# Two attention units of tiles 2 and 3 share a lot for their scores in a one-core hybrid decoder step

## The chip, the cores and the metric

One core of a Trainium2 chip. The metric is the device time of one execution in microseconds (us), the median of several runs. The change is one table of numbers that places pieces of work in the kernel's written-out order; no instruction's shape changes.

## What is computed

The kernel does one inference step of a two-layer decoder on 512 prompt tokens (4 tiles of 128) and 8 sample tokens (a fifth, small tile). Layer 0 has differential attention, layer 1 a short gated convolution. Each is followed by a layer norm, an expert layer that looks 128 experts up for every token (8 heads, 16 experts each), another norm, and a gated embedding. What the change touches is the attention of the prompt tiles:

```
s = einsum('bqhcd,bkhcd->bchqk', q, k) * HD**-0.5 - slope * dist     # two score maps, c = 0, 1
p = softmax(s);  w = p[:, 0] - lam * p[:, 1]
o = einsum('bhqk,bkhv->bqhv', w, v)
```

and what it shares the engines with is the expert layer, whose rows `u_tab[idx]` and `v_tab[idx]` are gathered from HBM for every token:

```
a = einsum('td,thkd->thk', xt, u_tab[idx]);  hk = g * gelu(a)
out = einsum('thk,thkd->td', hk, v_tab[idx])
```

## The kernel before, in words

**Lots.** The expert layer sets the beat. One gather (`L989`, on GpSimd's queue) brings one expert row of u and v for each of a tile's 128 tokens, 128 x 2048 floats or 1 MB, into a ring of slots. Two gathers make a *lot*: VectorE takes the two dot products (`two_dots`, L1672, two of 128x1024), ScalarE the gelu, the gate and the scaling of the two v rows (`two_experts`, L1166 gelu, L1169, L1180), TensorE adds them into `acc` by 16 transposing products of 128x128 (`add_two`, L1919), which frees the two slots. A tile has 64 lots, so the lots of tiles 0 and 1 of layer 0 are counted 0 to 127 here. Up to gather 216 (lot 108) the ring has 8 slots, four lots: the gathers of lot t + 4 wait for the adds of lot t.

**Background.** All else (projections, attention, norms, routing for the next tile) stands in lots as *pieces*, in an order that `Plan.build` writes. TensorE does the pieces of lot t **before** its adds of lot t. ScalarE and VectorE do them **two lots behind** (`BEHIND = 2`): the pieces of lot t come after the expert work of lot t + 1 and before that of lot t + 2. Each engine works strictly in its order. A piece that ends in a PSUM bank takes the next of four banks in turn, so a product waits until the product four before it has been read (`bank_freed`); the reader is ScalarE or VectorE, in its own background.

**An attention unit** u is one head of one tile of 128 queries; units 16 to 23 are tile 2 and units 24 to 31 tile 3. It has four pieces:
- `score`: two products on TensorE (L1760), one bank each; VectorE adds the position bias and takes the maximum (L1334, L1342 twice, L1347), ScalarE two exponentials (L1070). Exp and gelu are in different function tables of ScalarE, so an `ACT_TABLE_LOAD` stands ahead of the exponentials and another ahead of the next gelu.
- `weigh`: VectorE combines the two maps (L1355, L1357, L1359).
- `w_turn`: TensorE transposes the weights, 3 or 4 blocks, into `tp` (L1771); ScalarE copies them (L1079). From unit 16 on all units use the same `tp` bank, so a unit's transposes wait for the copy of the unit before.
- `pv`: 3 or 4 products with the values (L1780), read by ScalarE (L1083, L1085).

From unit 16 on the score maps of units u and u - 2 share a buffer: VectorE's score step of u waits until TensorE has transposed u - 2 (`a_wT_ps`). Before the change the unit j of tile 2 has its scores in lot 36 + 7(j // 2) + 3(j % 2), that of tile 3 in lot 64 + 2j; `weigh` follows one lot later, `w_turn` four and `pv` seven. In the same lots lie the projections of tiles 2 and 3 (`qk` L1718, `v` L1752, `k_rows` L1731; up to lot 56), the routing of tile 1 (`route`, VectorE from L1502 to L1571), at lot 64 the change of tile (`back` L1981 and L1132, the copy of `acc` L1228), and at lots 72 and 90 the turning back of the heads (`o_back` L1787, L1092). The functions are `Plan.build`, and inside `build`: `logits`, `weights`, `lead`, `open_product`, `two_experts`, `add_two`.

Of the kernel before, what the change touches and what calls it, by code (L numbers as in the profile page):

```python
# [114 lines left out]
class Plan:  # L115
# [255 lines left out]
    def build(self):  # L371
# [71 lines left out]
        window(0, 1, (0, 10, r1[25:]), (14, 30, bg), (24, 32, r2[:13]))  # L443
        lots = steps[1][3] + steps[2][3]
        for j in range(HEADS):
            for b, at in ((2, 36 + 7 * (j // 2) + 3 * (j % 2)), (3, 64 + 2 * j)):
                u = b * HEADS + j
                lots[at] += self.score[u]
                lots[at + 1].append(self.weigh[u])
                lots[at + 4].append(self.w_turn[u])  # L450
                lots[at + 7].append(self.pv[u])
        for b, at in ((2, 68), (3, 86)):
            lots[at].append(self.o_root[b])
            lots[at + 1].append(self.o_scale[b])
# [1665 lines left out]
```

## Time and profile before

| | |
|---|---|
| median of 3 runs | 3188.34 us (3184.56 to 3188.4) |
| the profiled execution's own time | 3192.09 us |
| its span, first to last instruction | 3190.1 us |
| granted TensorE clock, mean | 0.874 |
| busy: TensorE, VectorE, ScalarE, GpSimd | 77%, 71%, 62%, 38% |
| DMA: mean rate, share of the gather queue | 394 GB/s, 84.9% |
| chain that ended last: DMA, TensorE, VectorE, ScalarE | 37%, 25%, 17%, 11% |
| `ACT_TABLE_LOAD` ahead of gelu, whole run | 111 of 1283 ns |
| ScalarE in a lot: gelu; two gates; two scalings | 203 ns; 286 ns each; 1141 ns each |
| VectorE in a lot: two dot products | 1222 ns each |

A time in the profile is counted from the span's start. Lot 36 begins (its first dot product) at 465.9, lot 64 at 639.7, lot 84 at 751.3. PE is TensorE, DVE VectorE, ACT ScalarE, POOL GpSimd. "[x <-y]" behind a row is how long the engine stood idle before it and what ended that.

### The profile page before, as it was taken

To read this page: it belongs to the slowest core of one execution; us is meant where nothing else is said; L and a number is where in the kernel's file an instruction comes from. 1 tells how busy PE (TensorE), PEld (TensorE's weight loads), DVE (VectorE), ACT (ScalarE), POOL (GpSimd) and SP (SyncE) were. 2 spreads that over 40 slices of the span, in tenths; PEclk is the share of its full clock that TensorE was granted. 3 is DMA by queue.
4 is the path that set the end of the run, shared out by engine and by line. 5 is a ranking of instruction groups with operands and counts; after the bars stand their busy time and mean duration, and the time that the engine had idled before them with its cause. 6 is when DMAs were issued, how large, how long until landed. Compare 5 with 4: busy or idle time off the path is not lost.

```text
span 3190.1 us, 42742 instructions
## 1 busy us (share of the span) xinstructions
PE 2449.7 (77%) x13752; PEld 2024.4 (63%) x13752; DVE 2259.8 (71%) x5825; ACT 1989.4 (62%) x3694; POOL 1221.5 (38%) x1095
## 2 busy tenths in 40 slices
PE   8886878766978777886877687888787565587777
PEld 6555767655777666775765566776576555546665
DVE  2625678886467877778856877677668888678655
ACT  1325567797566865556655796555656666657883
POOL 1113333434444443343434344334444444444341
PEclk9878989887989889898888898998799877877899
DMA  7558999989999999999999999999999999999996
GB/s 291 185 215 354 397 418 406 401 364 405 411 419 420 421 420 421 421 420 416 383 420 421 382 421 421 421 420 421 418 419 420 405 422 420 414 375 421 421 421 278
DMA packets 182544, 1256.05 MB, mean 394 GB/s; under 512 B 21359, under 2 KB 26223, under 8 KB 33585
## 3 DMA queue, kind: packets, MB, share of 16 engines
q0 software_dynamic: 156320, 1113.83, 84.9%
q1 hardware_dynamic: 24416, 136.35, 10.7%
q10 hardware_dynamic: 1584, 3.15, 0.3%
q8 instruction: 110, 1.80, 0.2%
q14 instruction: 114, 0.93, 0.1%
HBM read 1246.78 MB, written 6.50 MB: 393 GB/s over the span
## 4 chain that ended last, share of the span: by engine, by line
DMA 37%; PE 25%; DVE 17%; ACT 11%; issue 4%; DVEq 3%; ACTq 2%; POOL 1%; SPq 0%; POOLq 0%
DMA arena<-in_uv,idx 35%; DVE arena L1672 9%; PE acc L1919 8%; PE bank L1946 6%; ACT arena L1180 5%; PE bank L1937 4%; PE bank L1718 2%; PE bank L1752 1%; DMA panel<-in_panels 1%; POOL arena L989 1%; DVEq L1578 1%; ACT act_w L1169 1%; ACT L1166 1%; ACTq L1167 1%; ACT L1159 1%
## 5 line engine op out<-in xcount | busy, mean ns | idle before, releaser
L989 POOL DMA_INDIRECT arena<-in_uv,idx x1024 | 1176.1, 1149 | 1724.2 <-PE acc L1919 1496.9
L1919 PE MATMUL acc<-cst,arena 128*128 128x128 f32 x8128 | 1245.7, 315 | 631.5 <-ACT arena L1180 630.8
L1919 PEld LDWEIGHTS acc<-cst,arena 128*128 128x128 f32 x8128 | 1094.2, 163 | 804.2 <-ACT arena L1180 777.4
L1672 DVE CUSTOM_DVE_ANT_0 arena<-arena,h 128x1024 f32<-128x1024 f32 x1024 | 1230.3, 1222 | 491.5 <-DMA arena<-in_uv,idx 484.0
L1180 ACT ACTIVATE arena<-arena,act_w 128x1024 f32<-128x1024 f32 x1016 | 1112.0, 1141 | 37.0 <-issue 2.4
L1166 ACT ACTIVATE act_w<-dots 128x2 f32<-128x2 f32 x520 | 105.3, 203 | 840.0 <-DVE dots L1672 839.0
L1946 PE MATMUL bank<-hT,panel 128*128 128x264 f32 (+2 forms) x1856 | 431.5, 389 | 6.5 <-issue 6.5
L1946 PEld LDWEIGHTS bank<-hT,panel 128*128 128x128 f32 x1856 | 352.4, 201 | 58.4 <-issue 8.9
L1169 ACT ACTIVATE act_w<-act_w 128x1 f32<-128x1 f32 x1040 | 249.5, 286 | 44.3 <-issue 2.2
L1166 ACT ACT_TABLE_LOAD x111 | 142.4, 1283 | 1.6
L1718 PE MATMUL bank<-hT,panel 128*128 128x264 f32 (+1 forms) x512 | 120.7, 397 | 19.1 <-DMA panel<-in_panels 13.6
L1718 PEld LDWEIGHTS bank<-hT,panel 128*128 128x128 f32 x512 | 100.5, 199 | 35.9 <-DMA panel<-in_panels 14.4
L1937 PE MATMUL bank<-panel,qT 128*128 128x256 f32 (+1 forms) x448 | 108.7, 399 | 0.0
L1937 PE MATMUL bank<-panel,hT 128*128 128x256 f32 (+1 forms) x448 | 102.9, 384 | 0.7 <-ACT hT L1126 0.7
L1937 PEld LDWEIGHTS bank<-panel,qT 128*128 128x128 f32 (+1 forms) x448 | 82.1, 189 | 19.3 <-issue 3.3
L1937 PEld LDWEIGHTS bank<-panel,hT 128*128 128x128 f32 (+1 forms) x448 | 70.5, 162 | 25.1 <-issue 4.8
L1672 DVE DVE_READ_ACCUMULATOR2_ANT dots<- 128x1 f32 x1040 | 85.2, 82 | 0.0
L1502 DVE COPY yb<-tp 128x256 f32<-128x256 f32 x80 | 33.8, 422 | 65.1 <-PE tp L1861 60.8
L1937 PE MATMUL bank<-panel,arena 128*128 128x256 f32 x256 | 62.4, 403 | 7.5 <-DMA panel<-in_panels 6.7
L1070 ACT ACTIVATE h<-h,small 128x128 f32<-128x128 f32 (+3 forms) x64 | 35.4, 554 | 50.7 <-DVE small L1347 50.4
L1551 DVE TENSOR_TENSOR yb<-ya,cst 128x512 f32<-128x512 f32 x80 | 55.4, 692 | 11.4
L1937 PEld LDWEIGHTS bank<-panel,arena 128*128 128x128 f32 x256 | 51.3, 204 | 16.6 <-DMA panel<-in_panels 7.5
(241 smaller groups left out, 2262.2 us busy)
## 6 DMA issues: line engine op xcount, KB each, us to landing
panel<-in_panels SPq DMA_DIRECT2D x116, 1024.0 KB, 9.3
arena<-in_uv,idx POOLq DMA_INDIRECT x1024, 19.9
arena<-in_cache_k POOLq DMA_DIRECT2D x16, 512.0 KB, 6.6
arena<-in_cache_v POOLq DMA_DIRECT2D x16, 512.0 KB, 4.8
arena<-out_y_s POOLq DMA_DIRECT2D x8, 512.0 KB, 9.0
arena<-in_panels SPq DMA_DIRECT2D x4, 1024.0 KB, 8.2
h<-in_h SPq DMA_DIRECT2D x2, 1024.0 KB
out_y_p<-h SPq DMA_DIRECT2D x3, 512.0 KB
```

Of the source, the lines that this page charges most:

```text
L989: nc.gpsimd.indirect_dma_start(uv[:, slot_of(e), :], None, uv_dram[layer], bass.IndirectOffsetOnAxis(ids[:, r:r + 1], 0)).then_inc(gathere ...
L1070: e = nc.scalar.activation(logit(u)[:, c, 0:n], logit(u)[:, c, 0:n], ACT.Exp, bias=nb[:, u % 2, c:c + 1], scale=SCALE, accum_out=lsum[:, u ...
L1166: nc.scalar.activation(act_w[:, 1, half, s], dots[:, half, s], ACT.Gelu).then_inc(gelu_done, 1)
L1169: nc.scalar.activation(act_w[:, 2, half, r:r + 1], act_w[:, 1, half, r:r + 1], ACT.Copy, scale=act_w[:, 0, half, r:r + 1])
L1180: nc.scalar.activation(row, row, ACT.Copy, scale=act_w[:, 2, half, r:r + 1]).then_inc(weighted, 1)
L1502: V.tensor_copy(r_sc, tp[0][:, 0:256]).then_inc(sc_read, 1)
L1551: V.tensor_tensor(r_eq.rearrange("p (k i) -> p k i", i=16), r_ijf.rearrange("p (k i) -> p k i", i=1).broadcast_to([P, 32, 16]), const("iot ...
L1672: V.tensor_tensor_reduce(uv[:, slot_of(e), 0:D], uv[:, slot_of(e), 0:D], x_rows, 1.0, 0.0, ALU.mult, ALU.add, dots[:, G % 2, r:r + 1]).the ...
L1718: t = mm(product_of[:, 0:width], w[:, c, :], hT[:, c, 0:width], start=(c == 0), stop=(c == C - 1))
L1919: m = mm(acc[:, c * P:(c + 1) * P], uv[:, slot_of(e), D + c * P:D + (c + 1) * P], const("ident"), is_transpose=True, start=False, stop=Tru ...
L1937: last = mm(bank[0:m, x.n % BANKS, 0:PW], src[:, c, first:first + m], weights[:, c, :], start=(c == 0), stop=(c == chunks - 1))
L1946: last = mm(bank[:, x.n % BANKS, 0:width], w[:, c, :], hT[:, c, lo:lo + width], start=(c == 0), stop=(c == C - 1))
```

## The change

The scores of units 2i and 2i + 1 of a tile are placed in the same lot: in tile 2 in lots 36, 43, 50, 57 (the second unit three lots earlier than before), in tile 3 in lots 64, 68, 72, 76 (the second two lots earlier, and each later pair spread over four lots as before). Their `weigh` pieces share the next lot. `w_turn` and `pv` come four and seven lots behind the scores for the first unit, five and eight for the second.

```diff
         for j in range(HEADS):
-            for b, at in ((2, 36 + 7 * (j // 2) + 3 * (j % 2)), (3, 64 + 2 * j)):
+            for b, at in ((2, 36 + 7 * (j // 2)), (3, 64 + 4 * (j // 2))):
                 u = b * HEADS + j
                 lots[at] += self.score[u]
                 lots[at + 1].append(self.weigh[u])
-                lots[at + 4].append(self.w_turn[u])
-                lots[at + 7].append(self.pv[u])
+                lots[at + 4 + j % 2].append(self.w_turn[u])
+                lots[at + 7 + j % 2].append(self.pv[u])
```

TensorE in tile 3, lots 71 to 76 (L1780 `pv`, L1771 `w_turn`, L1760 scores, L1787 `o_back`, L1919 the adds, 16 to a lot, L1861 routing):

```order
 L1780 MATMUL bank<-arena,weights_t 128x128 x4
 L1919 MATMUL acc<-cst,arena 128x128 x16
+L1780 MATMUL bank<-arena,weights_t 128x128 x4
 L1771 MATMUL tp<-cst,h 128x128 x4
-L1760 MATMUL bank<-qT,arena 128x512 x2
+L1760 MATMUL bank<-qT,arena 128x512 x4
 L1787 MATMUL bank<-cst,x_sample 128x128 x8
 L1919 MATMUL acc<-cst,arena 128x128 x16
+L1771 MATMUL tp<-cst,h 128x128 x4
+L1919 MATMUL acc<-cst,arena 128x128 x16
+L1861 MATMUL tp<-keys,qT 128x128 x2
+L1919 MATMUL acc<-cst,arena 128x128 x16
```

Lot 72 now opens with a `pv` and holds four score products, so its last score product takes the bank of that `pv`, of the same lot; the second unit's transposes stand behind the adds of lot 72.

ScalarE at the same place, before:

```order
L1079 ACTIVATE weights_t<-tp 128x512
L1070 ACT_TABLE_LOAD
L1070 ACTIVATE h,small<-h,small 128x512 x2
L1206 ACTIVATE act_w<-gate 128x8
L1166 ACT_TABLE_LOAD
L1166 ACTIVATE act_w<-dots 128x2
```

and with the change (L1092 reads `o_back`):

```order
L1083 ACTIVATE lnb<-bank,small 128x128
L1085 ACTIVATE bank,sums<-bank,small 128x128
L1079 ACTIVATE weights_t<-tp 128x512
L1070 ACT_TABLE_LOAD
L1070 ACTIVATE h,small<-h,small 128x512 x4
L1092 ACTIVATE arena<-bank,small 128x4x128 x2
L1166 ACT_TABLE_LOAD
```

Four exponentials stand behind one table load where two stood; in ScalarE's whole order there are 217 table loads where there were 233.

TensorE in tile 2, lots 50 to 54, before (L1718 `qk`, L1731 `k_rows`):

```order
L1780 MATMUL bank<-arena,weights_t 128x128 x3
L1771 MATMUL tp<-cst,h 128x128 x3
L1760 MATMUL bank<-qT,arena 128x384 x2
L1919 MATMUL acc<-cst,arena 128x128 x16
L1718 MATMUL bank<-hT,panel 128x256 x16
L1919 MATMUL acc<-cst,arena 128x128 x32
L1718 MATMUL bank<-hT,panel 128x256 x8
L1780 MATMUL bank<-arena,weights_t 128x128 x3
L1760 MATMUL bank<-qT,arena 128x384 x2
L1919 MATMUL acc<-cst,arena 128x128 x16
L1861 MATMUL tp<-keys,qT 128x128 x2
L1718 MATMUL bank<-hT,panel 128x256 x8
```

and with the change:

```order
L1780 MATMUL bank<-arena,weights_t 128x128 x3
L1760 MATMUL bank<-qT,arena 128x384 x4
L1919 MATMUL acc<-cst,arena 128x128 x16
L1718 MATMUL bank<-hT,panel 128x256 x16
L1780 MATMUL bank<-arena,weights_t 128x128 x3
L1919 MATMUL acc<-cst,arena 128x128 x32
L1718 MATMUL bank<-hT,panel 128x256 x8
L1919 MATMUL acc<-cst,arena 128x128 x16
L1861 MATMUL tp<-keys,qT 128x128 x2
L1718 MATMUL bank<-hT,panel 128x256 x8
```

The `pv` and the two scores that stood in lot 53 are gone from it. The last `qk` product, in lot 54, took the bank of the `qk` of lot 53; now it takes that of the first `qk` of lot 51.

## Rows read from the trace of the kernel before

**Rows 1.** The page, GB/s moved in 40 slices of 80 us.
```profile
GB/s 291 185 215 354 397 418 406 401 364 405 411 419 420 421 420 421 421 420 416 383 420 421 382 421 421 421 420 421 418 419 420 405 422 420 414 375 421 421 421 278
```

**Rows 2.** Windows: stretch, length, busy time of each engine (x instructions), clock, DMA share, GB/s.
```profile
497.00:560.00 63.00, 58.20 (x351) 51.53 (x352) 50.82 (x144) 50.04 (x98) 21.61 (x20) 0.97 1.00 402
560.00:640.00 80.00, 61.84 (x377) 53.64 (x375) 65.99 (x196) 63.97 (x125) 31.72 (x27) 0.87 0.98 401
640.00:700.00 60.00, 40.94 (x256) 34.61 (x255) 49.95 (x127) 57.62 (x105) 24.42 (x20) 0.83 0.87 353
700.00:756.00 56.00, 38.20 (x248) 33.62 (x247) 42.95 (x109) 53.11 (x106) 21.65 (x22) 0.86 0.98 390
756.00:800.00 44.00, 27.17 (x148) 24.20 (x147) 20.73 (x33) 27.40 (x50) 19.01 (x17) 0.73 1.01 422
...
591.00:602.00 11.00, 11.00 (x72) 10.08 (x71) 8.84 (x26) 9.06 (x17) 4.81 (x4) 1.00 0.81 300
...
650.00:655.00 5.00, 4.31 (x24) 4.31 (x25) 3.63 (x10) 4.95 (x13) 0.50 (x1) 0.66 0.06 25
```
The engines of these rows are PE, PEld (its weight loads), DVE, ACT and POOL.

**Rows 3.** Groups by line, ScalarE, 466 to 756: busy us, mean ns | idle before.
```profile
L1070 ACT ACT_TABLE_LOAD x16 | 20.5, 1283 | 0.3
```

**Rows 4.** Timeline of tile 3's units, 697 to 723: start, us, engine, line, operation.
```profile
697.60 1.28 ACT L1070 ACT_TABLE_LOAD   x1
...
704.39 0.42 DVE L1502 COPY yb<-tp 128x256 f32<-128x256 f32 x1
...
706.52 0.42 DVE L1334 TENSOR_SCALAR pTs<-lng 128x512 f32<-128x512 f32 x1
...
708.67 1.23 DVE L1672 CUSTOM_DVE_ANT_0 arena<-arena,h 128x1024 f32<-128x1024 f32 x1
...
709.92 1.28 ACT L1070 ACT_TABLE_LOAD   x1
...
711.21 0.72 ACT L1070 ACTIVATE h<-h,small 128x512 f32<-128x512 f32 x1
...
712.76 0.17 DVE L1355 RECIPROCAL small<-small 128x2 f32<-128x2 f32 x1 [1.70 <-ACT h L1070]
...
714.24 1.23 DVE L1672 CUSTOM_DVE_ANT_0 arena<-arena,h 128x1024 f32<-128x1024 f32 x1
...
718.47 2.19 ACT L1180 ACTIVATE arena<-arena,act_w 128x1024 f32<-128x1024 f32 x2
...
720.46 1.91 PE L1919 MATMUL acc<-cst,arena 128*128 128x128 f32 x16
...
721.16 1.28 ACT L1070 ACT_TABLE_LOAD   x1
...
722.21 0.60 PE L1771 MATMUL tp<-cst,h 128*128 128x128 f32 x4
...
722.74 1.13 PE L1760 MATMUL bank<-qT,arena 64*128 64x512 f32 x4
```
A product of 512 columns is recorded as two parts, so x4 is two products.

**Rows 5.** Timeline of lot 72, TensorE: the second half of `o_back`.
```profile
694.24 1.12 PE L1787 MATMUL bank<-cst,x_sample 128*128 128x128 f32 x4 [4.29 <-ACT bank L1085]
```

**Rows 6.** Timeline of lot 64, the change of tile.
```profile
650.69 1.19 PE L1780 MATMUL bank<-arena,weights_t 128*128 128x128 f32 x6 [3.38 <-ACT h L1132]
...
654.50 0.94 POOL L989 DMA_INDIRECT arena<-in_uv,idx  x1 [10.50 <-PE acc L1919]
```

**Rows 7.** Timeline of lots 50 to 54, to the gather of lot 58.
```profile
562.13 1.97 PE L1919 MATMUL acc<-cst,arena 128*128 128x128 f32 x16
...
564.42 0.34 ACT L1083 ACTIVATE x_sample<-bank,small 128x128 f32<-128x128 f32 x1
...
574.47 3.62 PE L1718 MATMUL bank<-hT,panel 128*128 128x256 f32 x16
...
585.47 5.38 PE L1718 MATMUL bank<-hT,panel 128*128 128x256 f32 x16 [3.52 <-issue]
...
592.76 1.98 POOL L989 DMA_INDIRECT arena<-in_uv,idx  x1 [8.66 <-PE acc L1919]
```

## The prediction

> **What bounds the kernel now.** I read the 40 slices first. The DMA engines move 418 to 422 GB/s wherever nothing holds them up, and the attention of tiles 2 and 3 lies in slices that show 406, 401, 364 and 405 [rows 1]. So the gathers set the time of most of the kernel, and what is worth something here is a *hole*: time in which the DMA engines lack work. Next come the windows of these lots. Against 421 GB/s, the four stretches from 497 to 756 lose 63 x 19/421 = 2.8, 80 x 20/421 = 3.8, 60 x 68/421 = 9.7 and 56 x 31/421 = 4.1 us, 20.4 us in all; from 756 on the rate is 422 again [rows 2]. **20.4 us is the most that this change can give**, and only a delay that makes a new hole can cost.
>
> In tile 2 (497 to 640) no engine is full, VectorE and ScalarE are at 80% and TensorE at 92% and 77%. In tile 3 (640 to 756) ScalarE is busy 57.6 of 60 and 53.1 of 56 us [rows 2]: it is the bound, and VectorE, at 50.0 of 60, is next. The timeline then shows where the three large holes come from. One is at 591 to 602 (300 GB/s, 11 x 121/421 = 3.2 us), one at 650 to 655 (25 GB/s, 4.7 us) [rows 2]. In each the gather queue stood for 8.7 and 10.5 us on TensorE's adds [rows 6, 7], and TensorE on a PSUM bank that ScalarE had not yet read: that is how a wait in the background becomes a hole.
>
> **What the change removes.** Each of the 16 units has its own load of the exp table, 1.283 us [rows 3], and a load of the gelu table, as long, behind its exponentials. With two units to a load, 8 of each go: 16 x 1.283 = 20.5 us of ScalarE, half of it in tile 2 and half in tile 3. In tile 2 ScalarE is not the bound; its load time is hidden by the gathers. In tile 3 two units (four lots) take 697.60 to 709.92 to 721.16, that is 12.32 + 11.24 = 23.6 us with `o_back` or 2 x 11.24 = 22.5 without [rows 4]. Less 2.57 us it would be 19.9, which is also what eight gathers of 1.05 MB take at 421 GB/s (8 x 2.49 = 19.9). This is the gain if nothing else happens: of the three pairs that end before the DMA takes over again about 7.7 us.
>
> The Trainium skill prices a switch higher: "ScalarE: Activation LUTs", section "What ACT_TABLE_LOAD costs", adds about 1.38 us of drain to the 1.283 us load. By it the 16 switches would be worth an estimated 42.6 us. The trace disagrees: the load that starts at 709.92 is followed by the exponential at 711.21, 1.29 us later [rows 4], so I charge the load alone.
>
> **What it adds, waits, tile 3.** Two rules of the order now meet.
> - Lots 72 and 76 (and 50, 57, 43, 64) have their fourth score product on a bank that a product of the same lot fills (`pv`, or `back` at 64). ScalarE reads that only after the expert work of the *next* lot. TensorE's adds of the lot stand behind this.
> - VectorE's score step of a pair's second unit waits for the transposes of the unit two before, and these stand one lot later, behind those adds.
>
> I count from the end of ScalarE's scaling of lot 73. ScalarE reads the `pv` of lot 72: 0.7. Last score product 0.6 (half of 1.13 [rows 4]). `o_back`: eight transposes, 1.8 (four took 1.12 after a wait [rows 5], and the other four follow at about the 0.60 of a `w_turn`). Adds 1.9. Transposes 0.6. Score step of the second unit 2.15 (706.52 to 708.67), of which 1.7 is behind the wait [rows 4, 5]. Sum 0.7 + 0.6 + 1.8 + 1.9 + 0.6 + 1.7 = 7.3. Then VectorE alone: dots of 74 2.3 (2 x 1.23, less overlap), two weighings of 1.48 (712.76 to 714.24), dots of 75 2.3, routing of 2.13 (704.39 to 706.52), dots of 76 and 77 4.6 [rows 4]: 14.3, together 21.6. ScalarE follows VectorE (from the dots of 76, done at 19.3: lot 76 in 3.1, being gelu, two gates and the scaling of 2.19 [rows 4]; the `pv` 0.7; lot 77 in 3.0): **26.1 us for the pair, against 23.6**. For lot 76 the same count without `o_back` (5.5 up to the score step, then the same pieces, 14.3, and 3.0 of ScalarE behind the last dots) gives 22.8 against 22.5. The pair at lot 68 has no such bank, but its second transposes wait for ScalarE's copy of the first, after lot 69: about 0.6 of the 2.57 is lost, -1.9. At lot 64 TensorE has two more score products, 1.1, behind the 3.38 us wait [rows 6] and one `w_turn` fewer, 0.6: +0.5. Sum for tile 3: 0.5 - 1.9 + 2.5 + 0.3 = +1.4.
>
> TensorE's clock makes this worse. In the stretch of the hole at 650 the granted clock is 0.66, between 1.2 and 2.4 GHz, and a `qk` product that follows a wait of 3.52 us takes 5.38 us, where the one before it took 3.62 [rows 2, 7]. The four TensorE steps above, 4.9 us, stand behind a wait of three us and more. At half clock throughout they would cost 4.9 more in each of two pairs. Since the row of 5.38 is half way between, and VectorE hides some of it, I take 1.6 for both together. **Tile 3: +3.0 us.** Its bounds: -7.7 (the loads alone; of the waits nothing reaches the path) and +1.4 + 9.8 = +11.2.
>
> **Tile 2.** At lot 50 the same bank wait appears: the last score product waits for the read that starts at 564.42 [rows 7] and takes 0.7, then come 0.6 of the product itself and 0.2 of signals, so the adds begin at about 565.9, where they begin at 562.13 now: +3.8. The gathers are well ahead at this place, so nothing goes idle. Behind it TensorE has lots 51 to 54, and there the wait of 3.52 us before the last `qk`, and the slow 5.38 instead of 3.62, go away [rows 7], 5.3 us, because this bank is now read long before. What remains on TensorE's path is +3.8 - 5.3 and the transposes of unit 19, 0.5, which left lot 50 for lot 48: the gather of lot 58 starts about **2.0 us earlier** than 592.76, in front of a hole of 3.2 us. It then passes lot 57, whose bank wait delays the gather of lot 61 by about 3 us; there the DMA has panels and stores queued, so I cost it at nothing (without that cover: +3). At lot 43 the bank wait exists already, by the order; the two more score products fall into it, 0 to +0.6, given back by the load that goes. **Tile 2: -2.0 us**; bounds -6.6 (both stretches without holes) and +3.8 + 3.0 = +6.8.
>
> **Sum.** -2.0 + 3.0 = +1.0 on the profiled execution, whose span is 3190.1 and own time 3192.1, so 3193.1 there. The runs lie lower: their median is 3188.34, and +1.0 gives **3189**. About 0.2%, 6.4 us, is what a measurement of this kernel can tell from no change. The work of POOL's and SP's queues keeps its order; the load of h that waits for the last transposes is free to start one lot earlier, and I cost it at nothing, since DMA-bound lots follow.
>
> **Rivals.**
> - *The loads win* (faster). VectorE's late score step is absorbed, since it has 17% idle in tile 3 [rows 2], and the pairs run at 19.9. Then tile 3 gives -7.7 and tile 2 -2.0: 3178.6. For it: ScalarE at 96% and the 1.70 us in which VectorE waits for the exponentials [rows 4]. Against it: two pairs out of four have a wait of about 7 us in the middle. The Trainium skill's rule to group calls by table set ("ScalarE: Activation LUTs", "Table sets: the hidden batching unit") is on this side.
> - *The bank waits win* (slower). Mechanism: lots 72 and 76, TensorE's adds behind ScalarE's read, at the low clock. Price: the full +11.2 of tile 3, less 2.0: 3197.5. It decides as soon as the second unit's score step starts over 7 us behind the dots of the next lot. Lot 72 already has TensorE waiting 4.29 us for ScalarE to read a bank [rows 5]. The Trainium skill's page "TensorE: Matmul & The Clock Gate", section "HAM oscillation", says that waits between bursts put the array back to the slow clock, which the 0.66 above bears out.
> - *Nothing reaches the end*: the gathers hide both signs, 3188.
>
> **How the numbers follow.** Forecast 0.42, nothing at all 0.16, the loads 0.18, the bank waits 0.24. Forecast and nothing are within 0.2%, the others mostly outside: faster 0.18, same 0.58, slower 0.24. The range takes in either rival's time and leaves out what lies beyond: 3178 on one side, and on the other 3199, 1.5 past the bank waits.
>
> **What would show it.** ScalarE's table loads 233 down to 217. In tile 3 loads of exp about 20 us apart if the loads win, 23 to 26 if not; TensorE waiting some 3 us before its last score product in lots 72 and 76, and VectorE some 5 us before L1342 at lots 72 and 76. The hole at 591 to 602 filled, the `qk` of lot 54 at 3.6 us with no wait, the hole at 650 still there. I am wrong if the time of lot 64 is not 1 to 4 us earlier, or that of lot 84 more than 6 us off the present 751.3.

## The result, and the profile of the changed kernel

The changed kernel takes **3203.61 us** (median of 6 runs, 3200.17 to 3206.07), the kernel before 3187.2 on the same chip: ratio **1.005**, 95% interval 1.004 to 1.006. It is 16 us slower, and above the range that I gave (3178 to 3199). The profiled execution took 3204.46 us, its span 3202.3, 12.2 over before's; it reached lot 36, up to which the orders are the same, 4.7 us earlier (461.2 for 465.9).

The page, GB/s in 40 slices of 80 us, answers to [rows 1]: the slices of tiles 2 and 3, the seventh to the ninth, have gone from 406 401 364 to 391 385 327.

```profile
GB/s 296 182 232 357 401 419 391 385 327 387 420 418 421 417 420 421 421 419 421 375 420 422 386 418 421 421 421 421 420 419 420 406 418 421 416 376 421 421 421 274
```

The windows of [rows 2] again, with the columns named there, and three new ones behind them:

```profile
497.00:560.00 63.00, 55.61 (x318) 48.28 (x316) 47.15 (x133) 41.33 (x87) 20.44 (x18) 0.92 0.94 383
560.00:640.00 80.00, 62.21 (x365) 55.52 (x366) 65.69 (x196) 57.97 (x116) 28.32 (x26) 0.85 0.96 385
640.00:700.00 60.00, 39.36 (x227) 32.13 (x225) 46.62 (x122) 48.55 (x96) 22.82 (x19) 0.80 0.88 344
700.00:756.00 56.00, 36.60 (x224) 32.14 (x225) 38.80 (x99) 42.78 (x90) 21.61 (x18) 0.82 0.83 321
...
590.00:602.00 12.00, 12.00 (x82) 11.07 (x80) 8.46 (x26) 7.78 (x17) 4.48 (x5) 1.00 1.01 417
...
566.00:576.00 10.00, 10.00 (x50) 9.17 (x50) 8.98 (x24) 7.42 (x17) 2.89 (x2) 0.87 0.86 333
...
602.00:625.00 23.00, 13.43 (x82) 11.11 (x81) 18.44 (x51) 15.08 (x32) 9.12 (x8) 0.81 0.93 356
```

The old hole at 591 to 602 is gone (417), as forecast, and two new ones stand beside it (333 and 356, where the same stretches before moved 422 and 407). In tile 3 ScalarE is no longer the bound: busy 42.8 of 56 us where it was 53.1. No engine replaced it. That is how a chain of waits looks in this view, with everybody idler and the DMA at 321.

ScalarE's groups by line, 466 to 756, answer to [rows 3]. Half of the loads are gone, as forecast (217 in the whole run):

```profile
L1070 ACT ACT_TABLE_LOAD x8 | 10.3, 1283 | 0.1
```

From the timeline, the first dot product of lot 36 starts at 461.2 (465.9 before), that of lot 64 at 638.5 (639.7) and that of lot 84 at 761.8 (751.3). So 3.5 us are lost from 36 to 64 and 11.7 from 64 to 84; behind that the change stays 10 to 12 us later by the span. In tile 3 the waits by engine and line show what took the place of the loads. First before, 640 to 756 (engine, what waited, for whom: total us, times, longest):

```profile
PE acc L1919 <- ACT arena L1180: 27.1, 8, 5.7
PE bank L1787 <- ACT bank L1085: 4.3, 1, 4.3
...
ACT act_w L1166 <- DVE dots L1672: 1.5, 2, 1.0
DVE h L1342 <- issue: 1.5, 8, 0.2
```

and with the change, the same window:

```profile
DVE h L1342 <- PE tp L1771: 15.2, 3, 7.2
ACT act_w L1166 <- DVE dots L1672: 12.7, 8, 3.7
PE tp L1771 <- ACT weights_t L1079: 9.2, 2, 4.9
...
PE bank L1760 <- ACT bank L1085: 5.6, 3, 2.4
PE bank L1760 <- ACT h L1132: 3.4, 1, 3.4
```

VectorE now waits 15.2 us for late transposes, TensorE 9.2 us for the copy out of the transposes' bank and 5.6 us for `pv` banks. The first and the last I had in the forecast; the second I had priced at about 0.6 us in one place.

The timeline of lot 72, which answers to [rows 4, 5], shows the first kind:

```profile
697.96 2.19 ACT L1180 ACTIVATE arena<-arena,act_w 128x1024 f32<-128x1024 f32 x2
...
700.80 1.22 PE L1760 MATMUL bank<-qT,arena 64*128 64x512 f32 x2 [2.23 <-ACT bank L1085]
...
701.96 1.97 PE L1787 MATMUL bank<-cst,x_sample 128*128 128x128 f32 x8
...
703.72 2.59 PE L1919 MATMUL acc<-cst,arena 128*128 128x128 f32 x16
...
705.71 0.94 POOL L989 DMA_INDIRECT arena<-in_uv,idx  x1 [8.96 <-PE acc L1919]
...
706.15 0.60 PE L1771 MATMUL tp<-cst,h 128*128 128x128 f32 x4
...
706.89 0.69 DVE L1342 CUSTOM_DVE_ANT_0 h<-bank,pTs 128x512 f32<-128x512 f32 x1 [7.25 <-PE tp L1771]
...
708.50 0.72 ACT L1070 ACTIVATE h<-h,small 128x512 f32<-128x512 f32 x1 [4.43 <-DVE small L1347]
```

ScalarE's scaling ends at 700.1, the `pv` is read by 700.8, then the last score product, `o_back`, the adds, the transposes, and VectorE starts at 706.89: 6.7 us behind the scaling, where I had counted 5.6 (7.3 less the 1.7 of the step itself). The gather of lot 76 stood 8.96 us on these adds.

The timeline of lots 68 and 69 shows the kind that I had underrated:

```profile
674.69 0.57 ACT L1079 ACTIVATE weights_t<-tp 128x512 f32<-128x512 f32 x1
...
675.41 1.09 PE L1771 MATMUL tp<-cst,h 128*128 128x128 f32 x4 [4.88 <-ACT weights_t L1079]
...
676.29 3.62 PE L1919 MATMUL acc<-cst,arena 128*128 128x128 f32 x16
676.58 0.72 ACT L1070 ACTIVATE h<-h,small 128x512 f32<-128x512 f32 x1
676.64 0.69 DVE L1342 CUSTOM_DVE_ANT_0 h<-bank,pTs 128x512 f32<-128x512 f32 x1 [2.49 <-PE tp L1771]
...
678.13 1.23 DVE L1672 CUSTOM_DVE_ANT_0 arena<-arena,h 128x1024 f32<-128x1024 f32 x1
678.48 1.69 POOL L989 DMA_INDIRECT arena<-in_uv,idx  x1 [5.94 <-PE acc L1919]
```

The pair's transposes share one bank and stand one lot apart, while ScalarE copies two lots behind. So TensorE waits almost a whole lot of ScalarE with lot 69's adds behind it; these then run at the lower of the two clocks (3.62 us for 16, where the row of [rows 4] has 1.91; the granted clock from 676.29 to 679.91 is 0.50, that is 1.2 GHz), and the dots of lot 70 start at 678.13.

Tile 2, lots 50 and 57, answers to [rows 7]:

```profile
563.31 1.64 PE L1760 MATMUL bank<-qT,arena 64*128 64x384 f32 x2 [3.67 <-ACT bank L1085]
...
564.88 3.67 PE L1919 MATMUL acc<-cst,arena 128*128 128x128 f32 x16
...
585.18 3.62 PE L1718 MATMUL bank<-hT,panel 128*128 128x256 f32 x16
...
608.64 1.64 PE L1760 MATMUL bank<-qT,arena 64*128 64x384 f32 x2 [4.44 <-ACT bank L1085]
610.21 3.28 PE L1919 MATMUL acc<-cst,arena 128*128 128x128 f32 x16
...
612.45 1.79 POOL L989 DMA_INDIRECT arena<-in_uv,idx  x1 [7.87 <-PE acc L1919]
```

The `qk` of lot 54 has no wait and 3.62 us, as forecast. But the adds of lots 50 and 57 take 3.67 and 3.28 us instead of 1.97 [rows 7] and 1.9, which I had left out, and both times the rate falls behind them, as the windows show.

### The profile page after: what moved, and what is told of

Read it like the earlier page. It is cut to its first block, busy times and chain, and to the rows that moved or that the text cites. A ratio compares the mean times of both kernels' runs of the same rounds, so it can differ in the third digit from the quotient of the medians.

```text
span 3202.3 us, 42726 instructions
## 1 busy us (share of the span) xinstructions
PE 2451.4 (77%) x13752; PEld 2029.1 (63%) x13752; DVE 2260.4 (71%) x5825; ACT 1969.8 (62%) x3678; POOL 1211.6 (38%) x1095
## 4 chain that ended last, share of the span: by engine, by line
DMA 37%; PE 24%; DVE 18%; ACT 11%; issue 4%; DVEq 3%; ACTq 2%; POOL 1%; SPq 0%; POOLq 0%
DMA arena<-in_uv,idx 35%; DVE arena L1672 9%; PE acc L1919 8%; ACT arena L1180 6%; PE bank L1946 5%; PE bank L1937 4%; PE bank L1718 2%; DMA panel<-in_panels 1%; ACT act_w L1169 1%; ACTq L1167 1%; DVEq L1578 1%; ACT L1166 1%; POOL arena L989 1%; ACT L1159 1%; PE bank L1752 1%
## 5 line engine op out<-in xcount | busy, mean ns | idle before, releaser
L1919 PE MATMUL acc<-cst,arena 128*128 128x128 f32 x8128 | 1246.9, 316 | 624.3 <-ACT arena L1180 623.6
L1919 PEld LDWEIGHTS acc<-cst,arena 128*128 128x128 f32 x8128 | 1097.5, 164 | 791.1 <-ACT arena L1180 764.4
L1946 PEld LDWEIGHTS bank<-hT,panel 128*128 128x128 f32 x1856 | 347.8, 198 | 56.4 <-issue 7.5
L1718 PE MATMUL bank<-hT,panel 128*128 128x264 f32 (+1 forms) x512 | 117.7, 389 | 13.3 <-DMA panel<-in_panels 13.3
L1718 PEld LDWEIGHTS bank<-hT,panel 128*128 128x128 f32 x512 | 98.2, 194 | 29.0 <-DMA panel<-in_panels 14.1
L1937 PEld LDWEIGHTS bank<-panel,hT 128*128 128x128 f32 (+1 forms) x448 | 71.2, 164 | 23.7 <-issue 2.9
L1937 PEld LDWEIGHTS bank<-panel,arena 128*128 128x128 f32 x256 | 50.3, 200 | 16.6 <-DMA panel<-in_panels 7.7
```

Source lines behind the costliest of these rows:

```text
L1718: t = mm(product_of[:, 0:width], w[:, c, :], hT[:, c, 0:width], start=(c == 0), stop=(c == C - 1))
L1919: m = mm(acc[:, c * P:(c + 1) * P], uv[:, slot_of(e), D + c * P:D + (c + 1) * P], const("ident"), is_transpose=True, start=False, stop=Tru ...
L1937: last = mm(bank[0:m, x.n % BANKS, 0:PW], src[:, c, first:first + m], weights[:, c, :], start=(c == 0), stop=(c == chunks - 1))
L1946: last = mm(bank[:, x.n % BANKS, 0:width], w[:, c, :], hT[:, c, lo:lo + width], start=(c == 0), stop=(c == C - 1))
```

## Experiments

Every run (5 to 12 executions) is set against executions of before on the same chip. A time "over before" is the ratio times 3188, with its 95% interval in brackets. As a second reading, the time from lot 64 to lot 88 (first dot products, timeline) is given for tile 3: **137.0 us before, 149.0 in the change**. It is of one execution each. The same reading from lot 36 to 64 varied from 173.4 to 178.1 among five kernels with the same order in tile 2, so I don't rest anything on it there. The whole of 64 to 88 is steadier where the order of tile 3 is before's (137.0, 136.2 in `t2_pairs`, 136.7 in `t2_early`), but its parts are not: lots 64 to 68 took 22.5, 22.8 and 24.3 us in these three, 68 to 72 22.7, 21.3 and 20.5.

### Which tile

Tile 2 alone in pairs, and tile 3 alone. Against the change, first `t2_pairs`, then `t3_pairs` (in both the new `j % 2` of `w_turn` and `pv` is kept for the paired tile only):

```diff
-            for b, at in ((2, 36 + 7 * (j // 2)), (3, 64 + 4 * (j // 2))):
+            for b, at in ((2, 36 + 7 * (j // 2)), (3, 64 + 2 * j)):
...
+            for b, at in ((2, 36 + 7 * (j // 2) + 3 * (j % 2)), (3, 64 + 4 * (j // 2))):
```

> Pairs in tile 2 alone; tile 3 as before. The change cost 16 us in all; between lot 36 and lot 64 it lost 3.5 us and between lot 64 and lot 84 11.7 us against before. If the two tiles add, this run is 3 to 5 us over before. My own sum had tile 2 at -2.0. If instead the later gathers of tile 2 push work into tile 3 (tile 3 depends on how it is entered), this run holds more than 6 us of the loss.

> Pairs in tile 3 alone; tile 2 as before. If the two tiles add, this run is 10 to 13 us over before, and lots 72 and 76 show the same waits of TensorE and VectorE as in the changed kernel. If the loss in tile 3 needs the late gathers of tile 2, it is under 6 us.

Measured: tile 2 alone **+3.8** (1.0 to 6.7), ratio 1.0012; tile 3 alone **+18.5** (14.3 to 22.6), ratio 1.0058. Tile 3 is most of it. It came out over the 10 to 13 that I expected, though its stage (150.8) is 13.8 over before, and the two tiles add up to 22.3 where the change has 15.9 (12.8 to 19.1); how far they really add is not settled by these intervals.

### Transposes earlier, values' products earlier

The first edit is `turn_early`; the other two together are `pv_early3`, the last alone `o_back_74`.

```diff
-                lots[at + 4 + j % 2].append(self.w_turn[u])
+                lots[at + 3 + j % 2].append(self.w_turn[u])
...
-                lots[at + 7 + j % 2].append(self.pv[u])
+                lots[at + 7 + j % 2 - (b == 3)].append(self.pv[u])
...
-            lots[at + 4] += self.o_back[b]
+            lots[at + (6 if b == 2 else 4)] += self.o_back[b]
```

> The changed kernel with both transposes of a pair one lot earlier (three and four lots behind the scores), the products with the values left where they are. The second unit's transposes now stand ahead of the scores of the next pair in tile 3, so VectorE's score step no longer waits for transposes behind the adds; the bank wait of the fourth score product stays. If VectorE's late score step is what costs (the wait of 5 to 7 us before L1342 in lots 72 and 76), the run returns to 4 to 7 us over before, and that wait shrinks under 2 us. If the bank wait is what costs, because the adds and so the slots come late, the run stays 12 us or more over before. No table load comes back in either case (217).

> The changed kernel; in tile 3 the products with the values one lot earlier (six and seven lots behind the scores), the turning back of tile 2's heads at lot 74. Transposes stay where the change has them, tile 2 too. So no lot from 68 on has a score product on the bank of a product of its own lot (one stays on a bank of the lot before), and VectorE's score step still waits for transposes of the next lot. If the two waits add, this takes away what the earlier transposes did not: some 5 us, to 10 to 12 us over before. If the late transposes are harmful only because they stand behind adds that wait for the bank, it takes nearly all of tile 3's loss: 3 to 6 us over before. If it stays at 14 or more, the bank is not what holds the adds.

> The changed kernel with one edit: the two products that turn the heads of tile 2 back stand in lot 74 in place of 72. Bringing tile 3's products with the values one lot forward together with this edit gave back 11.6 us of the 16.4. If the turning back of the heads was much of that (1.8 us of transposes at the slow clock between the late score product and the adds of lot 72), this run is 4 us or more under the changed kernel, 12 us over before or less. If the products with the values on the banks of the scores were it, this run stays at 14 to 17 us over before.

Measured: earlier transposes **+11.2** (7.0 to 15.3), lots 64 to 88 in 143.1; values' products earlier **+4.8** (1.6 to 8.0), 139.4; `o_back` alone moved **+16.9** (12.1 to 21.4), 148.8. The earlier transposes landed between my two expectations, and their 4.7 us against the change lie within the noise; they took VectorE's 15.2 us of waits away, but TensorE's for the copy rose from 9.2 to 12.2. `o_back` is innocent, and the place of `pv` (moved together with `o_back`) is worth 11 us, clear of the intervals. The timeline of lot 72 with `pv` earlier shows why it is worth so much more than its wait:

```profile
702.02 1.12 PE L1760 MATMUL bank<-qT,arena 64*128 64x512 f32 x2 [0.77 <-ACT bank L1085]
...
703.08 1.97 PE L1919 MATMUL acc<-cst,arena 128*128 128x128 f32 x16
...
705.59 0.63 PE L1771 MATMUL tp<-cst,h 128*128 128x128 f32 x4 [0.55 <-ACT weights_t L1079]
...
706.36 0.69 DVE L1342 CUSTOM_DVE_ANT_0 h<-bank,pTs 128x512 f32<-128x512 f32 x1 [2.03 <-PE tp L1771]
```

The bank wait fell from 2.23 to 0.77 us, and VectorE's wait behind it from 7.25 to 2.03. The late transposes do their harm behind late adds. The copy's wait is still in this run (8.8 us), and lots 68 to 72 still take 27.0 us; but lots 76 to 84 take 38.8, less than before's 42.6. So what the pair at lot 68 loses is largely given back once the bank waits of lots 72 and 76 are short.

### The bank wait alone

Transposes in tile 3 two and four lots behind the scores, all else as in the change.

```diff
-                lots[at + 4 + j % 2].append(self.w_turn[u])
+                lots[at + 4 + j % 2 - (b == 3) * (2 - j % 2)].append(self.w_turn[u])
```

> The changed kernel with one edit, in tile 3: transposes two and four lots behind the scores. Neither the copy out of the transposes' bank (9.2 us of TensorE's waits in the change) nor VectorE's wait for late transposes (15.2 us) is left; the bank waits of lots 72 and 76 and the scores at lot 64 stay, and tile 2 is the change's (3.8 us over before). If the copy and the late transposes are the greater part of tile 3's loss and the bank wait does harm only through what stands behind it, this run is 3 to 7 us over before. If the bank wait by itself costs the 11 us that the run with the values' products one lot earlier gave back, it is 10 us or more over before.

Measured **+12.1** (7.3 to 16.6), 145.2. TensorE's wait for the copy and VectorE's for transposes are gone from the waits of 640 to 756; of the pieces' own waits these are the largest beside the 3.4 us of lot 64:

```profile
PE bank L1760 <- ACT bank L1085: 9.5, 4, 3.3
...
PE tp L1771 <- DVE h L1359: 4.9, 1, 4.9
DVE h L1342 <- PE bank L1760: 4.7, 3, 2.5
```

Less tile 2's 3.8 that is 8 us in tile 3, as the stage has it too (8.2 of 12.0), without the other two waits: the second expectation held for the total. VectorE then waits for the late score product itself. The bank wait is not quite alone, though: the banks' 9.5 us are more than the change's 5.6, the 4.9 us for VectorE's weighing are new, and lot 64 is as in the change. And 12.1 against the change's 15.9 lies within the noise, so the share of the other two waits is not shown by the times; by the stages, lots 68 to 72 fell from 26.4 to 23.7 us, which is what the copy cost there.

### Both early, and the start at lot 66

`early` has the first and the last edit; `early_66` the first and the second, with `o_back` at 72.

```diff
-                lots[at + 4 + j % 2].append(self.w_turn[u])
-                lots[at + 7 + j % 2].append(self.pv[u])
+                lots[at + 3 + j % 2].append(self.w_turn[u])
+                lots[at + 5 + j % 2].append(self.pv[u])
...
-            for b, at in ((2, 36 + 7 * (j // 2)), (3, 64 + 4 * (j // 2))):
+            for b, at in ((2, 36 + 7 * (j // 2)), (3, 66 + 4 * (j // 2))):
...
-            lots[at + 4] += self.o_back[b]
+            lots[at + (6 if b == 2 else 4)] += self.o_back[b]
```

> The changed kernel with transposes three and four lots behind the scores, the products with the values five and six behind, and the turning back of tile 2's heads two lots later (lot 74). In tile 3 no lot with scores then holds a product that ScalarE reads late, and no transposes stand behind the adds that the score step needs. If the two waits are the whole loss, the 8 saved table loads of tile 3 show and tile 3 ends 3 to 8 us earlier than before; tile 2 still has its bank conflicts at lots 43, 50 and 57 and may lose its 3.5. Total 3 us under to 2 us over before. If four score products and eight exponentials in one lot are too much for a lot whatever stands around them (slow clock, a lot of 7 us on ScalarE against four slots of gathers), the run stays 8 us or more over before.

> The kernel with both pieces early (three, four, five and six lots behind), and tile 3's pairs two lots later, at lots 66, 70, 74 and 78, so that no scores stand in the change of tile at lot 64; the heads of tile 2 are turned back at lot 72 as before. The early kernel lost 3.1 us against before between lots 64 and 68 and 0.3 us from there to lot 88. If that was the four score products on the banks of the two back products, this run is 3 us faster than it: 1 to 4 us under before. If the change of tile is slow whatever stands in it, it stays at 0 to 4 us over before.

Measured: **+3.5** (0 to 7.0), 140.3, and **+0.3** (-2.9 to 3.5), 140.2. The `pv` banks' waits are gone and nearly all of the loss with them, but no gain came from the loads, and `early` is a little over the range that I expected. (A pair has four exponentials; the eight in two of my expectations are a slip.) Whether lot 64 matters stays open: the intervals overlap and the stage is the same.

### What the loads are worth

The exponential of units 16 to 31 replaced, in before, in the change and in `early_66`. All three have 202 loads in the whole run, 31, 15 and 16 fewer than with the exponential (my expectations say 201 and 32), so they differ in the order alone. The identity takes as long as the exponential (713 and 714 ns for 128x512).

```diff
-                        e = nc.scalar.activation(logit(u)[:, c, 0:n], logit(u)[:, c, 0:n], ACT.Exp,
+                        e = nc.scalar.activation(logit(u)[:, c, 0:n], logit(u)[:, c, 0:n], ACT.Exp if u < 16 else ACT.Identity,
```

> The kernel before, with the exponentials of units 16 to 31 replaced by the identity function, of the same shape and the same two accumulated sums. It leaves out the exponential of tiles 2 and 3, and with it all 32 table loads around it (233 down to 201); no piece moves. If the loads were on the path in tile 3, as the rival in which the loads win has it, each pair of tile 3 is up to 5.1 us shorter until the gathers of four lots (19.9 us) bound it: 6 to 9 us under before. If the gathers and VectorE hide the loads, 0 to 3 us under before, and then the change had next to nothing to win with half of them.

> The changed kernel with the same replacement, 32 table loads fewer than before and 16 fewer than the change: what stands between this run and the last is the order of the pieces alone. If the waits of the order are the loss and the saved loads of the change were worth little, the difference between the two is 14 to 20 us. If ScalarE's time was what made the waits long (eight exponentials and two scalings in the lots behind the scores), removing more of it shrinks the difference to under 8 us.

> The kernel with early pieces and tile 3's pairs at lots 66 to 78, which had the time of before, with the exponentials of units 16 to 31 replaced by the identity (left out: the exponential of tiles 2 and 3, and so all 32 loads around it). Before with this replacement was 8.3 us under before. If the alternation of VectorE and ScalarE in a pair's lots, and not the loads, now sets tile 3, the last 16 loads are worth little here: 0 to 4 us under before, 4 to 8 over that run. If the paired order is as good as the unpaired one once its waits are gone, it comes down to 6 to 9 us under before.

| | with exp | without any load | 64 to 88 |
|---|---|---|---|
| before | 0 | **-8.3** (-11.5 to -4.8) | 137.0, 130.9 |
| the change | +15.9 | **+19.1** (14.3 to 23.6) | 149.0, 149.0 |
| `early_66` | +0.3 | **+5.1** (1.6 to 8.6) | 140.2, 141.0 |

In before's order 31 loads are worth 8.3 us (6.1 by the stage). In either of these paired orders the 15 or 16 that were left are worth nothing: ScalarE has idle time in each pair, and a load less makes it longer (in the change its waits for dots rose from 12.7 to 17.7 us, those for VectorE's maxima from 8.5 to 13.6). The difference of the order alone is 27 us, more than the change's loss and more than the 14 to 20 that I expected; `early_66` without loads, 5.1 over, lies outside both of its expectations.

### The last wait: the copy

In `early_66` what waits as it did not before is above all TensorE on the copy (15.1 us in four waits), and VectorE and ScalarE in turn. My theory at that point was the turns. Two runs move the first unit's transposes from three to two lots behind the scores, in `early_66` and in `spread_66` (which weighs the second unit one lot later). The first edit alone is `spread_66`, the second `early_turn2`, both `spread_turn2`.

```diff
-                lots[at + 1].append(self.weigh[u])
+                lots[at + 1 + j % 2].append(self.weigh[u])
...
-                lots[at + 3 + j % 2].append(self.w_turn[u])
+                lots[at + 3 + j % 2 - (b == 3) * (1 - j % 2)].append(self.w_turn[u])
```

> The kernel with early pieces and tile 3's pairs at lots 66 to 78, with the second unit's weighing on VectorE one lot later than the first (two lots behind the scores). In that kernel the pair's steps alternate: VectorE does two score steps, ScalarE waits, then does four exponentials while VectorE waits, then VectorE weighs twice while ScalarE waits for the next dot products. If this alternation is what eats the saved loads (worth about 4 us, half of the 8.3 that all 32 loads are), taking one weighing out gives 1 to 3 us back: 1 to 3 us under before. If VectorE's weighing is hidden, it stays at before, within 2 us.

> The kernel with early pieces and pairs at lots 66 to 78, and one edit in tile 3: the first unit's transposes two lots behind the scores in place of three, so that two lots lie between the transposes of a pair and not one. Both use one bank, and in that kernel TensorE waits 15.1 us in four waits for ScalarE to copy the first unit's weights out of it before it can transpose the second's, with the scores of the next pair and the adds behind. If these waits are what eats the saved loads, this run is 2 to 4 us under before. If the alternation of VectorE and ScalarE in a pair's lots sets tile 3, it is at before within 1.5 us although the waits for the copy are gone.

> The same edit on the kernel whose second unit is weighed one lot later (2.5 us under before, interval from 5.7 under to 1.0 over). If the waits for the copy (15.4 us there) are what is left, this run is 4 to 7 us under before. If not, it stays within 2 us of 3184, or is slower, where TensorE then waits two lots behind the scores for VectorE's first weighing.

Measured: `spread_66` **-2.5** (-5.7 to 1.0), 136.0. `early_turn2` **-5.7** (-9.2 to -1.9), ratio 0.9982, 132.6. `spread_turn2` **-12.1** (-16.3 to -8.0), 3176.32 us, ratio 0.9962, interval 0.9949 to 0.9975, 131.1. The last one beats both kernels and leaves nothing out. Its 12.1 us, from five runs (3174.66 to 3177.92), are more than the traces account for: its stage is 5.9 us shorter, and lots 36 to 100 take 369.4 us for 376.6. In its profiled execution 7.6 us more come from ahead of lot 36, where all orders are the same and where the 20 profiled executions differ by 9 us (lot 36 at 457.1 to 465.9). So that it is faster is shown, by 6 to 7 us in the stages; the rest may be chance.

Waits of 640 to 756, first `early_66`:

```profile
PE tp L1771 <- ACT weights_t L1079: 15.1, 4, 5.5
ACT act_w L1166 <- DVE dots L1672: 13.7, 7, 3.8
DVE h L1342 <- PE bank L1760: 9.3, 3, 3.7
```

then `early_turn2`:

```profile
PE tp L1771 <- DVE h L1359: 17.4, 4, 5.3
ACT act_w L1166 <- DVE dots L1672: 12.5, 6, 5.6
DVE arena L1672 <- DMA arena<-in_uv,idx: 11.8, 5, 3.7
```

ScalarE waits for dots as long as before the edit (12.5 and 13.7) and the time fell, so the turns were not what held the saved loads back. What the later weighing adds on top is not settled: alone it can't be told from before, and `spread_turn2` is 6.4 us under `early_turn2` in the medians but 1.5 in the stage. TensorE waits even longer, now for VectorE's weighing (L1359), but behind three of the four waits the adds stood another 0.1 to 2.3 us for ScalarE's scaling: they could not have run yet. What went is VectorE's wait for the next scores, 9.3 us, and in its place VectorE waits for the gathers: they are the bound again. One piece of each timeline, the second transposes and the scores behind them, lot 70 in `early_66` and then lot 74 in `early_turn2` (lot 74 in `early_66` has a wait of 2.20 and scores of 3.37 us):

```profile
672.41 1.09 PE L1771 MATMUL tp<-cst,h 128*128 128x128 f32 x4 [5.47 <-ACT weights_t L1079]
...
673.42 3.78 PE L1760 MATMUL bank<-qT,arena 64*128 64x512 f32 x8
```

```profile
690.00 0.60 PE L1771 MATMUL tp<-cst,h 128*128 128x128 f32 x4
...
690.53 1.99 PE L1760 MATMUL bank<-qT,arena 64*128 64x512 f32 x8
```

### The unpaired kernel, tile 2, and mixtures

`single_early`, against before:

```diff
-                lots[at + 4].append(self.w_turn[u])
-                lots[at + 7].append(self.pv[u])
+                lots[at + 3].append(self.w_turn[u])
+                lots[at + 5].append(self.pv[u])
```

`t2_early` is tile 2 of `early` with tile 3 of before; `t3_spread` tile 2 of before with tile 3 of `spread_66`; `single2_spread3` tile 2 of `single_early` with that same tile 3.

> The kernel before, unpaired, with its transposes three lots behind the scores and its products with the values five behind (it had four and seven). Before too had a bank wait in lots with scores (4.3 us before the last score product of lot 72, 3.4 at lot 64 and 3.5 at a projection of lot 54). If moving these reads off the lots with scores is worth something by itself, this run is 2 to 7 us under before, and the paired kernels should be compared with it, so that pairing is a loss even where its waits are removed. If pairing needs the early pieces and before does not, it is within 2 us of before.

> Pairs in tile 2 alone as in the run of tile 2's pairs, which was 3 us over before, but with transposes three and four lots behind the scores and the products with the values five and six. At lots 50 and 57 no score product is then on the bank of its own lot; lot 43 keeps two on a projection of values. If the bank waits at 50 and 57 are tile 2's loss, this run is at before or 1 to 2 us under. If the pairing itself costs there, it stays 2 to 4 us over.

> Tile 2 exactly as before; tile 3 in pairs at lots 66 to 78 with early pieces and the second weighing one lot later. The run with this tile 3 and paired tile 2 was 2.5 us under before (interval from 5.7 under to 1.0 over). If the gain is tile 3's loads and tile 2's pairing is neutral, this is 1 to 4 us under before. If tile 2's early pieces made it, this run is at before within 1 us.

> The same tile 3, with tile 2 unpaired and its pieces early (three and five lots behind the scores), so that both tiles are free of score products on banks of their own lot. The profiles gave the unpaired early tile 2 3 us and tile 3's spread pairs 2 us. If these add, this run is 3 to 6 us under before and the fastest kernel of all with its work complete. If the gathers give the time back, it is within 2 us of before.

(The 4.3 us of lot 72 stand before `o_back` [rows 5], not before a score product as the first of these says.) Measured: before with transposes 3 and `pv` 5 lots behind **-0.6** (-3.2 to 2.2); tile 2 in early pairs, tile 3 as before, **+0.6** (-2.5 to 3.8); tile 3 spread with before's tile 2 **0.0** (-3.5 to 3.2), and with an early unpaired tile 2 **-1.9** (-5.4 to 1.6). None can be told from before. No gain from early pieces shows in the unpaired order; transposes two lots behind were not tried in it, so what pairing itself gives to `spread_turn2` is not shown. Tile 2's early pairs were 3.2 us under its first pairs, which fits its bank waits, but the intervals overlap, so that is not shown.

## Why the prediction was wrong, point by point

- **The bound and the most that can be gained** (20.4 us, holes only): nothing contradicts it. The gathers are the bound where nothing waits, and `spread_turn2` won 6 to 7 of it by its stages, 12.1 by its median. (I wrote of three large holes and named two.)
- **The loads, 7.7 us in tile 3**: about right for the unpaired order (31 loads, in both tiles: 8.3 us). That a pair still gains 2.57 when it has a new wait was wrong: with a wait in the pair the loads are worth nothing (149.0 us with and without).
- **The pair at lot 68, "about 0.6 of the 2.57 is lost, -1.9"**: the term that was furthest off. From the first dots of lot 68 to those of lot 72 it took 26.4 us (663.4 to 689.8) against 22.7: +3.7, so 5.6 off. I had seen that the second transposes wait for ScalarE's copy, and priced what VectorE's step would be late by. But TensorE waited 4.88 us, the adds of lot 69 stood behind, and VectorE's two score steps, in one row, put the dots of lot 70 behind both. Without the copy's wait (transposes two and four behind) the same lots took 23.7, so it made 2.7 of the 3.7; in the rest VectorE waits for gathers, 3.4 us there for 1.8 before.
- **The pairs at lots 72 and 76, 26.1 and 22.8**: the mechanism and its order were right, the sizes short. Measured 28.6 (before 23.8) and 23.9 (before 21.3), so +4.8 and +2.6 where I had +2.5 and +0.3. TensorE's wait was 2.23 (I said some 3), VectorE's 7.25 and 5.50 (some 5). Lot 76 has two such waits, 0.96 and 2.39, as its third score product waits too. By the runs these two pairs decide the total: with their banks' waits taken out (`pv_early3`) the loss fell by 11 us, though the pair at lot 68 stayed slow.
- **Lot 64, +0.5**: to lot 68 it was +2.4. The four parts of the two last score products took 2.56 us behind the wait of 3.38 (I had 1.1), the six products behind them 1.65 for 1.19, and the gather of lot 68 stood 12.2 us where it had stood 10.50 [rows 6].
- **The clock, 1.6**: too small on the path that I counted, but not for a new reason. From TensorE's last score product to VectorE's step it took 6.1 us in lot 72, where I had 4.9, and 5.2 in lot 76, where I had 3.1: 3.3 more, twice the 1.6. The adds of these lots took 2.59 and 3.56 us; but they had taken 3.62 and 3.57 before, also behind waits. All adds of lots 64 to 82 took 51.0 us in the change and 48.6 before, so slow adds are at most a small part of tile 3's 11.7. In tile 2, where I had charged nothing, lots 50 and 57 had 3.67 and 3.28 for 1.97 and 1.9.
- **Sum of tile 3, +3.0**: measured +11.7, over my upper bound of 11.2. The pairs give 2.4 + 3.7 + 4.8 + 2.6 and lot 80 gives 1.8 back.
- **Tile 2, -2.0**: +3.8 (1.0 to 6.7). The hole at 591 to 602 was filled and the `qk` of lot 54 fast, both as said; the row of its 3.52 us names no bank, but the wait went with the order of the banks. "Nothing goes idle" at lot 50 and "the DMA has panels and stores queued" at lot 57 failed: 333 GB/s in 566 to 576 and 356 in 602 to 625. Half of a bound that I had written down, +6.8, was there.
- **The rivals**: "the bank waits win", 3197.5 with 0.24, was the right one in kind, 6 us short, because it kept tile 2 at -2.0. That its +11.2 for tile 3 is so near the measured 11.7 is luck: it had 12.6 for the pairs at 72 and 76, which cost 7.4, and -1.4 for lots 64 and 68, which cost 6.1. The Trainium skill's "TensorE: Matmul & The Clock Gate", section "HAM oscillation", stands on its side, and the adds of lot 69, behind 4.88 us of waiting, at a granted clock of 0.50, agree with it; the change's own cost does not rest on it, as the adds show. The Trainium skill's rule to group calls by table set ("ScalarE: Activation LUTs", "Table sets: the hidden batching unit") did not come out in the change (+15.9) or with both pieces early (+0.3). Grouped kernels that beat before are `early_turn2` and `spread_turn2`, and no run shows how much of their gain is the loads'.
- **What would have shown me wrong**: lot 64 was 1.2 us earlier by the span, within my 1 to 4, but by luck, since lot 36 was already 4.7 earlier; counted from lot 36 it was 3.5 later. A stage must be measured from its own first lot. Lot 84, 10.5 later, showed it plainly.

## What to carry to other kernels

A piece that one engine issues and another reads some lots later holds its bank for that whole lag; when pieces are moved together, list for each shared bank or buffer how many lots lie between the fill, the read and the next fill, and keep every such distance above the lag. Price a wait by what stands behind it on its own engine and then on the next, not by its own length: here 2.2 us of a bank wait stood ahead of 7.3 us on VectorE, and with 0.8 us in its place it was 2.0. And a saving on one engine was worth nothing here in an order with new waits, so first take the waits out, then batch: the same kind of pairs cost 16 us in one placing and were faster than before, by 6 us in the stage, in another.

## What the runs showed that I had not expected

- An engine that waits longer can be better: TensorE's waits before transposes rose from 15.1 to 17.4 us and the kernel became 6 us faster, since the wait moved to where the adds, three times of four, were not due.
- Taking the last 15 of these table loads out of the changed kernel did not make it faster (+19.1, 14.3 to 23.6, against +15.9).
- Behind waits of 2 to 6 us, 16 adds took up to 3.68 us for 1.91, in before as in the change, and in `early_66` four score products 3.78 for 1.99, at a granted clock of 0.50; the mean granted clock of the windows (0.80 and 0.82) hardly tells the change from before (0.83 and 0.86) [rows 2].
- Executions differ by up to 9 us ahead of lot 36, where every kernel has the same order: more than most of the effects looked for here, so a time of one execution says little unless it is cut into stages.
